# Forget sums by DMA, memory keys ahead of the conv mixer's projections, and sixteen more conv taps on TensorE, with a new order of the work behind them

## The reference

```python
log_f = jax.nn.log_sigmoid(fl.astype(jnp.float32) + b_forget.astype(jnp.float32))
cum = jnp.cumsum(log_f, axis=1).transpose(0, 2, 1)        # 8 heads x 512
...
    sb = (jnp.einsum('bhqd,bhkd->bhqk', sl(qb), kb).astype(jnp.float32) * scale
          + (c_q[..., None] - cum[:, :, None, :]))
    pb = jax.nn.softmax(jnp.where(causal, sb, -jnp.inf), axis=-1)
...
def pool_conv_mixer(h, w_in, pool_w, pool_scale, dw_w, dw_b, ln_g, ln_b, w_out):
    z = h @ w_in
    u, glu_a, glu_b = jnp.split(z, [POOL_W, POOL_W + CONV_W], axis=-1)
    pooled = jnp.stack([window_mean_minus_self(ug[:, :, i], w)
                        for i, w in enumerate(POOL_WINDOWS)], axis=2)
    ya = jnp.einsum("btgc,gcd->btgd", pooled, pool_w).reshape(b, t, POOL_W) * pool_scale
    gl = glu_a * jax.nn.sigmoid(glu_b)
    cv = causal_dwconv(gl, dw_w) + dw_b                   # 512 channels, 31 taps
    yb = jax.nn.silu(layernorm(cv, ln_g, ln_b))
    return jnp.concatenate([ya, yb], axis=-1) @ w_out
def memory_cross_attention(h, m, wq, wkv, wo):
    k, v = jnp.split(m @ wkv, 2, axis=-1)
...
```

## Time and profile before

| | us |
|---|---|
| median of 3 runs (lowest, highest) | 2516.14 (2513.30, 2516.99) |
| profiled execution | 2517.59 |
| its span | 2515.8 |
| PE busy in the span | 2422.4 (96%) |
| DVE, ACT, POOL busy | 1255.4, 962.2, 1002.8 |

### The profile page before, as it was taken

One profiled execution on the slowest core, in us unless ns is written; L12 is line 12 of the kernel. 1 busy time (PEld: TensorE's weight loads), 2 busy tenths in 40 slices (PEclk: granted clock), 3 DMA queues, 4 the chain that ended last, 5 costly groups with the idle time before them and its releaser, 6 DMA issues.

```text
span 2515.8 us, 30042 instructions
## 1 busy us (share of the span) xinstructions
PE 2422.4 (96%) x11158; PEld 1914.9 (76%) x11158; DVE 1255.4 (50%) x2109; ACT 962.2 (38%) x1439; POOL 1002.8 (40%) x744
## 2 busy tenths in 40 slices
PE   7999999999999999888999999999989999999998
PEld 6777667977888887756868888887556987888887
DVE  4453544324333336795347555556764324555555
ACT  4354334433322225523344222225766433322223
POOL 3323324242444453553515554454121142445443
PEclk9999999999999999998999999999999999999999
DMA  5222113431323222221312323222102331322331
GB/s 165 68 67 68 51 50 117 134 101 45 111 100 100 87 97 84 80 88 51 108 47 84 104 98 100 92 92 73 44 18 84 126 109 34 101 90 95 100 101 67
DMA packets 175563, 215.74 MB, mean 86 GB/s; under 512 B 6432, under 2 KB 157522, under 8 KB 175446
## 3 DMA queue, kind: packets, MB, share of 16 engines
q1 hardware_dynamic: 175446, 214.16, 26.2%
HBM read 212.04 MB, written 2.11 MB: 85 GB/s over the span
## 4 chain that ended last, share of the span: by engine, by line
PE 85%; DVE 9%; ACT 3%; issue 2%; POOL 1%; DMA 1%; DVEq 0%; SPq 0%; ACTq 0%
PE ps_l L771 74%; DVE arena L2327 3%; PE ps_l L984 3%; PE ps_l L1113 2%; PE ps_s L1040 2%; PE ps_l L893 2%; ACT w_hi L1306 1%; PE ps_s L1096 1%; POOL w_lo L622 1%; DVE arena L1852 1%; DVE a_lo L1858 1%; PE ps_s L999 1%; DVE x_T L2168 0%; DVE small L2546 0%; ACT arena L1333 0%
## 5 line engine op out<-in xcount | busy, mean ns | idle before, releaser
L622 POOL TENSOR_TENSOR w_lo<-w_raw,w_hi 128x512 fp32r<-128x512 f32 (+1 forms) x740 | 1002.6, 1387 | 1486.7 <-ACT w_hi L1306 1476.6
L771 PE MATMUL ps_l<-a_hi,w_hi 128*128 128x512 f32 x1936 | 768.3, 397 | 25.7 <-DVE b_lo L2186 16.0
L771 PE MATMUL ps_l<-a_lo,w_hi 128*128 128x512 f32 x1952 | 763.3, 392 | 0.0
L771 PE MATMUL ps_l<-a_hi,w_lo 128*128 128x512 f32 x1936 | 757.9, 391 | 0.0
L1306 ACT ACTIVATE w_hi<-w_raw 128x2048 fp32r<-128x2048 f32 x197 | 372.4, 1890 | 579.0 <-PE ps_l L771 560.3
L771 PEld LDWEIGHTS ps_l<-a_hi,w_hi 128*128 128x128 f32 x1936 | 366.1, 189 | 111.9 <-DVE b_lo L2186 16.7
L771 PEld LDWEIGHTS ps_l<-a_lo,w_hi 128*128 128x128 f32 x1952 | 369.6, 189 | 79.1 <-issue 2.9
L771 PEld LDWEIGHTS ps_l<-a_hi,w_lo 128*128 128x128 f32 x1936 | 365.5, 189 | 78.3
L771 PE MATMUL ps_l<-b_hi,w_hi 128*128 128x512 f32 (+1 forms) x908 | 337.1, 371 | 11.5 <-POOL w_lo L622 6.8
L771 PE MATMUL ps_l<-b_lo,w_hi 128*128 128x512 f32 (+1 forms) x908 | 334.8, 369 | 0.0
L771 PE MATMUL ps_l<-b_hi,w_lo 128*128 128x512 f32 (+1 forms) x908 | 334.8, 369 | 0.0
(11 more groups left out here) (272 smaller groups left out, 2629.3 us busy)
## 6 DMA issues: line engine op xcount, KB each, us to landing
w_raw<-in_ffn_w_up_dram SPq DMA_DIRECT2D x44, 1024.0 KB, 5.1
w_raw<-in_w_dram SPq DMA_DIRECT2D x32, 1024.0 KB, 5.2
w_raw<-in_ffn_w_down_dram SPq DMA_DIRECT2D x22, 1024.0 KB, 4.8
w_raw<-in_w_in_dram SPq DMA_DIRECT2D x20, 1024.0 KB, 5.4
w_raw<-in_xa_wkv_dram SPq DMA_DIRECT2D x16, 1024.0 KB, 5.6
w_raw<-in_w_kv_mem_dram SPq DMA_DIRECT2D x8, 1024.0 KB, 5.7
w_raw<-in_xa_wq_dram SPq DMA_DIRECT2D x8, 1024.0 KB, 5.0
w_raw<-in_xa_wo_dram SPq DMA_DIRECT2D x8, 1024.0 KB, 5.6
```

Of the source, the lines that this page charges most:

```text
L622: e.tensor_tensor(w_lo[:, b % 2, o], w_raw[:, b % 2, o], w_hi[:, b % 2, o].bitcast(F32), ALU.subtract).then_inc(w_lo_made[by], 1)
L771: ins = pe.matmul(o, *((v, w) if swap else (w, v)), start=first and n == 0, stop=last and n == 2)
```

## The change

1. **Forget sums.** The K matmuls and DVE's copies go. ACT writes `cum` to a DRAM buffer once, in its diff attention, and at each K event issues a DMA that reads one row of it back, broadcast to 128 partitions, into `nck`. DVE waits for it ahead of a head's first score.
2. **Memory keys.** `mem_rstd(1)` moves on ACT into the end of the MLP's loop; turns 0 and 1 of the memory stand ahead of the MLP's last projection, 2 and 3 behind it; three key blocks stand ahead of the sums and of glu, the fourth behind pool_u. ACT's and DVE's steps for them move with them (`last_z_and_keys`, `mem_keys` on DVE in two halves).
3. **Conv.** Of chunk 2, DVE does 15 taps and PE 16 (`conv2`), with the diagonals of `conv3` rewritten by ACT as they have been read. DVE adds the bank of conv2 to its own sum. DVE's taps fall from 93 to 77 and the counts at which it turns to other work are new.
4. **Order behind.** pc_out_a's second block stands between ln_mean and ln_var, and the four value blocks stand together behind ln_var. ACT and DVE follow.

The engines' rows, each in its program's order; the names are out<-in, and xN counts like rows.

ACT at the start of fox attention, before: the last high part of diff attention (L1466), then the exponentials of head 0 (L1499).

The diff, cut:

```diff
@@ -271,19 +270,23 @@
         for f in range(nf):
             if f + 1 < nf:
                 ups(f + 1)
+            elif name == "mlp":
+                L.add("memT1", "vv")
             put(down, 2, 1024, 256 * f, 0, "v" * 8)
         L.base[name + "_last"] = len(L.who) - 8
     mlp("mlp", FF1 // 256, [("w1", 0, "v")], "v", "w2")
     norm(3)
     norm(4, "v")
+    L.add("memT1+", "vv")
+    feat("xk1", "xa_wkv_2:0", "a", [0, 256, 512])
     feat("glu", "pc_w_in_2", "v", [512, 1024, 768, 1280])
-    L.add("memT1", "vvvv")
     feat("pool_u", "pc_w_in_2", "v", [0, 256])
-    keys(1, "xa_wkv_2:0")
+    feat("xk1+", "xa_wkv_2:0", "a", [768])
     L.add("pool_w", "vvvv")
     feat("pc_out_a", "pc_w_out_2", "v", [0, 512], nk=4, width=512)
     S.add("conv3", "v")
+    S.add("conv2", "v")
     S.add("ln_mean", "v")
     S.add("ln_var", "a")
     for j in range(4):
...
@@ -321,15 +324,17 @@
 TWO_PI = (6.28125, 2029 * 2.0 ** -20, 2 * np.pi - 6.28125 - 2029 * 2.0 ** -20)
 PI32 = 3.1415925
 PE_Q = 3
+SHARED_Q, SHARED_TAPS = 2, 15
 def tap_order():
...
@@ -1026,12 +1035,6 @@
                       turned=causal_turn(U["diff"], lambda h, i: s_diff(i, 0)), subln=diff_subln,
                       fills={"qk_b": feat_fill("qk_b", 8, 256, xa), "v_b": tok_fill("v_b")})
-            def fox_keys(g, h):
-                claim(pe, S, g)
-                pe.wait_ge(cum_ready, 2)
-                pe.matmul(bank(S, g)[:, :], ident[0:8, h:h + 1].to_broadcast([8, P]), cum, start=True, stop=True)\
-                    .then_inc(s_full, 1)
-
             def masked_score(g, i, pairs):
...
@@ -1149,6 +1152,9 @@
                     if f + 1 < nf:
                         ups(b, g)
                         down(f, b + n_up, g + 2 * n_up)
+                    elif name == "mlp":
+                        mem_turn(1, (0, 1))
+                        down(f, b, g + 2)
                     else:
                         down(f, b, g)
@@ -1159,16 +1165,20 @@
                 norm(3)
                 norm(4)
-            stage("glu", xa, ready=h_ready(4), behind={0: both_sums})
-            mem_turn(1)
+            mem_turn(1, (2, 3))
+            mem_keys(1)
+            both_sums()
+            stage("glu", xa, ready=h_ready(4))
             stage("pool_u", xa, nb=2)
-            mem_keys(1)
+            stage("xk1+", xm, nb=1, n=MEM)
             g = S.base["conv3"]
             claim(pe, S, g)
             pe.wait_ge(glu_r, 4)
             for j in range(CONV_K):
                 pe.wait_ge(diag_r, j + 1)
                 ins = pe.matmul(bank(S, g)[:, :], diag(j), gl[:, PE_Q, j:j + T], start=j == 0, stop=j == CONV_K - 1)
+                if j < CONV_K - 1:
+                    ins.then_inc(diag_read, 1)
             ins.then_inc(s_full, 1)
             g = L.base["pool_w"]
             pe.wait_ge(ld_pw, 16)
@@ -1177,23 +1187,30 @@
                 pe.wait_ge(pool_r, q + 1)
                 pe.matmul(bank(L, g + q)[:, :], pool_wt[:, q, :], window[q][:, 16:UW], start=True, stop=True)\
                     .then_inc(l_full, 1)
...
-            stage("pc_out_a", lambda k: xa(4 + k), nk=4, c=512, nb=2,
-                  ready=lambda k: wait_read(pe, L, L.base["pool_w"] + k))
+            g = S.base["conv2"]
+            claim(pe, S, g)
+            for j in range(SHARED_TAPS, CONV_K):
+                pe.wait_ge(diag_r, CONV_K + j - SHARED_TAPS + 1)
+                ins = pe.matmul(bank(S, g)[:, :], diag(j - SHARED_TAPS), gl[:, SHARED_Q, j:j + T],
+                                start=j == SHARED_TAPS, stop=j == CONV_K - 1)
+            ins.then_inc(s_full, 1)
+            b, g = plan.block_base["pc_out_a"], L.base["pc_out_a"]
+            feat(b, g, 4, 512, lambda k: xa(4 + k), lambda k: wait_read(pe, L, L.base["pool_w"] + k))
             g = S.base["ln_mean"]
             claim(pe, S, g)
             pe.wait_ge(tap, TAPS)
-            wait_read(pe, S, S.base["conv3"])
+            wait_read(pe, S, S.base["conv2"])
             for q in range(4):
                 ins = pe.matmul(bank(S, g)[:, :], ones[:, :], cvt[:, q, :], start=q == 0, stop=q == 3)
             ins.then_inc(s_full, 1)
-            mem_values(1, 0)
+            feat(b + 1, L.base["pc_out_a"] + 4, 4, 512, lambda k: xa(4 + k))
             g = S.base["ln_var"]
             claim(pe, S, g)
             for q in range(4):
                 pe.wait_ge(ln_sq, q + 1)
                 ins = pe.matmul(bank(S, g)[:, :], ones[:, :], ly[:, q, :], start=q == 0, stop=q == 3)
             ins.then_inc(s_full, 1)
-            for j in (1, 2, 3):
+            for j in range(4):
                 mem_values(1, j)
             stage("pc_out_b", xa, nk=4, c=512, nb=2, ready=lambda k: pe.wait_ge(yb_lo, k + 1))
             cross(1, 5)
...
@@ -1431,6 +1448,15 @@
                 act.activation(pt(h)[:, 0:i + 1, i * P:(i + 1) * P], tiles, ACT.Copy).then_inc(l_free["a"], 1)
+            def sums_row(h):
+
+                act.wait_ge(ld_sums, 16)
+                if h < 2:
+                    act.wait_ge(sub_n, 3 + h)
+                else:
+                    wait_read(act, S, plan.events["fox"][1]["S", h - 2, TT - 1])
+                act.dma_start(nck[:, h % 2, :], sums_d[h:h + 1, :].to_broadcast([P, T])).then_inc(ld_sums, 16)
...
@@ -1453,6 +1479,9 @@
                     copy_turned(g, h, i)
                 if kind == "O":
                     wait_group(act, L, g)
+                    if h == 0:
+                        act.wait_ge(cum_ready, 2)
+                        act.dma_start(sums_d, cum).then_inc(ld_sums, 16)
                     if h >= 2:
                         wait_group(act, S, at["M", h - 2, 0])
...
                     square(k, n, g)
-            def mlp(k_norm, after):
+            def last_z_and_keys():
+
+                g = L.base["mlp_last"]
+                mem_parts(1, range(4))
+                for n in range(KD - 1):
+                    z_hi(4, n, g)
+                hi(plan.block_base["xk1"] + 1)
+                mem_parts(1, range(4, KD))
+                z_hi(4, KD - 1, g)
+                for n in range(KD):
+                    square(3, n, g)
+                    square(4, n, g)
+                    if n in (1, 5):
+                        key_copies(1, n // 4)
+                key_copies(1, 2)
+
+            def mlp(k_norm):
                 b0, g0 = plan.block_base["mlp"], L.base["mlp"]
                 norm_rstd(k_norm)
                 u = UPB["mlp"]
...
+
+            def shared_diags():
+
+                for j in range(SHARED_TAPS, CONV_K):
+                    act.wait_ge(diag_read, j - SHARED_TAPS + 1)
+                    w = COL["conv_dw_w_2"] + 4 * j + SHARED_Q
+                    act.activation(diag(j - SHARED_TAPS), ident, ACT.Copy, scale=cols[:, w:w + 1]).then_inc(diag_r, 1)
             g, b = L.base["glu"], plan.block_base["glu"]
             for pair in (0, 1):
...
@@ -2334,19 +2396,18 @@
             glu_in(1, 1)
             taps(18)
             glu(1)
-            mem_keys(1)
             normed_x(range(4, KD))
             scaled(L.base["pool_u"], 2, lambda j: up_[:, j, 16:UW], r34)
+            taps(26)
+            scaled(L.base["pool_u"] + 2, 2, lambda j: up_[:, 2 + j, 16:UW], r34)
             taps(28)
-            scaled(L.base["pool_u"] + 2, 2, lambda j: up_[:, 2 + j, 16:UW], r34)
-            taps(40)
             wait_read(dve, L, L.base["pool_u"] + 3)
             for n, (dst, src) in enumerate(((pw_a, up_), (pw_b, pw_a[:, 1:4]), (pw_a[:, 2:4], pw_b[:, 1:3]),
...
@@ -2355,7 +2416,7 @@
             for q, w in enumerate(WINDOWS):
                 dve.scalar_tensor_tensor(out=window[q][:, 16:UW], in0=window[q][:, 16:UW], scalar=1.0 / w,
                                          in1=up_[:, q, 16:UW], op0=ALU.mult, op1=ALU.subtract).then_inc(pool_r, 1)
-            taps(76)
+            taps(60)
             for q in range(4):
                 g = L.base["pool_w"] + q
                 wait_group(dve, L, g)
...
                                          in1=A_hi[:, 4 + q, :].bitcast(F32), op0=ALU.mult, op1=ALU.subtract)\
                     .then_inc(l_free["v"], 1)
-            dve.wait_ge(x_normed, 8)
-            for n in range(KD):
-                taps(76 + 2 * (n + 1))
-                g = L.base["pc_out_a"] + n
-                wait_group(dve, L, g)
-                dve.tensor_tensor(x[:, n, :], bank(L, g)[:, :], x[:, n, :], ALU.add).then_inc(l_free["v"], 1)
             taps(TAPS)
             g = S.base["conv3"]
             wait_group(dve, S, g)
             dve.tensor_scalar(cvt[:, PE_Q, :], bank(S, g)[:, :], col("conv_dw_b_2", PE_Q), None, ALU.add)\
                 .then_inc(s_free["v"], 1)
+            g = S.base["conv2"]
+            wait_group(dve, S, g)
+            dve.wait_ge(tap, TAPS)
+            dve.tensor_tensor(cvt[:, SHARED_Q, :], cvt[:, SHARED_Q, :], bank(S, g)[:, :], ALU.add)\
+                .then_inc(s_free["v"], 1)
+
+            def pool_out(ns):
+                for n in ns:
```

(7 more changed lines are left out.)

130 lines of the change are left out of this document (71 added, 59 removed).

## The result

The changed kernel takes 2480.54 us (median of four runs, 2478.91 to 2481.74) where the kernel before takes 2515.32 beside it: 34.8 us less, a ratio of 0.986 with a 95% interval of 0.985 to 0.987. The prediction was 2484, with 2476 to 2497 as its range. The profiled execution took 2479.44 us, its span 2477.5, against 2517.59 and 2515.8.

What follows compares the result with a forecast made beforehand. PE's own queue bounds the fox stretch; the conv stretch is PE work plus waits, mostly on DVE's tap queue, and half clock. Fox -8.4 and conv -23.8 give -32.2 us: median 2516.14 to 2484, range 2476 to 2497.

Steps and rivals of the forecast that it cites:

- Fox sums: Fox attention: eight K events leave PE's full queue at 1.05 us each, 8.4 us gained.
- the cover: Fox attention: slack of 13.0 us before DVE reads head 1's row and 10.4 behind; PE waits from 23.4.
- The landing: Fox attention: time from issue until a broadcast row arrives, 2.9 or 5.2 us, with 5.2 taken as nearer.
- Head: Start of the conv stretch, keys ahead of sums: PE waits 1.7, 0.8 and 2.4 us; the 8.1 us keys' wait goes.
- one spell: Conv stretch: one spell of PE at half clock, 1.7 us (none to two: 0 to 3.4).
- Conv, PE: Conv stretch: sixteen taps move from DVE to PE at 0.86 us each, adding 13.7 us of PE work.
- Conv, DVE: Conv stretch: DVE's queue of 47.7 us plus 15.7 beside POOL; margins one to two before pool_w, 3 before ln_mean.
- Rival B: Conv stretch: DVE stays the bound, all 20 POOL pieces cost it 1.27 us; 2488 to 2496 us, chance 0.26.
- Behind: Behind the conv, pc_out_a to xv3: PE waits of 1.6, 0.4 and 0.8 us, where before had 2.1 and 0.8.
- Sum: Conv stretch: PE work 177.8 + 13.7, waits 7.7, spell 1.7, together 200.9 against 224.7 us; with fox -32.2.

Runs made afterwards that it cites:

- the kernel with the old order: Changed kernel with the whole old order behind the conv on PE, ACT and DVE; sums by DMA, keys at the head and conv2 stay: 2494.05 us.
- conv taps only: Kernel before with only the 16 taps of chunk 2 on PE behind pool_w, nothing else moved: 2510.20 us, ratio 0.9975.
- sums and keys: Kernel before with forget sums by DMA and keys at the head, all conv taps on DVE and old order behind: 2498.34 us, ratio 0.9932.
- both of the old order: Changed kernel with the old order behind the conv, put back on PE alone (2490.34 us) or on PE, ACT and DVE (2494.05 us).
- the kernel with late rows: Changed kernel with each head's row issued only directly ahead of that head's first exponential: 2479.38 us, ratio 0.9857.
- the kernel with 14 taps: Changed kernel with 17 taps of chunk 2 on DVE and 14 on PE, instead of 15 and 16: 2479.76 us, ratio 0.9855.

## Why the prediction was right

**Fox sums, -8.4.** The term is exact, the cover as read. The landing I had placed near 5.2 us was 3.0 to 3.4.

**Head.** I had waits of 1.7, 0.8 and 2.4 us; they are 1.5, 0.7 and 1.8, at the same three places and with the same releasers, and no spell of half clock follows. The sum had its one spell, 1.7 us, here behind the sums' wait, since I took POOL's 2.3 us as the shortest wait of before that a spell followed. That was misread: xv3's 7.52 us in the earlier trace rows follow a wait of 2.08, as the timeline of the kernel before has it:

```profile
1194.04 0.39 PE L771 MATMUL ps_l<-w_hi,b_hi 128*128 128x256 f32 x1 [2.08 <-POOL w_lo L622]
```

ACT's mem_rstd fits into its idle time: it ends at 946.1, with the next operand waited for behind it, and PE doesn't wait.

**Conv, PE.** conv2 took 13.9 us for 13.7 forecast, ln_mean and ln_var 3.60 each.

**Conv, DVE.** From the first gate product to the last window product I had 63.4 us, and it took 64.4 (1030.29 to 1094.75). I counted 15 or so POOL pieces beside it; all 20 were, at 0.8 us each on average, 17 in all. It left 0.6 us of margin ahead of pool_w instead of 1 to 2, and 2.9 instead of 3 ahead of ln_mean. The timeline of DVE in the changed kernel:

```profile
1072.74 6.78 DVE L2389 SCALAR_TENSOR_TENSOR arena<-arena,cols 128x512 f32<-128x512 f32 x4
...
1082.22 2.73 DVE L2389 SCALAR_TENSOR_TENSOR arena<-arena,cols 128x512 f32<-128x512 f32 x4
```

and of POOL:

```profile
1044.41 17.63 POOL L633 TENSOR_TENSOR w_lo<-w_raw,w_hi 128x512 fp32r<-128x512 f32 x8 [6.29 <-ACT w_hi L1323]
1065.20 15.44 POOL L633 TENSOR_TENSOR w_lo<-w_raw,w_hi 128x512 fp32r<-128x512 f32 x8 [3.16 <-ACT w_hi L1323]
```

The first piece of the 17.63 us, in a window of its own:

```profile
1044.41 6.43 POOL L633 TENSOR_TENSOR w_lo<-w_raw,w_hi 128x512 fp32r<-128x512 f32 x1 [6.29 <-ACT w_hi L1323]
```

Four taps take 6.78 us beside POOL and 2.73 without, and POOL's eight pieces 15.44 and 17.63 us where four alone take 5.03: each side is held up by the other. Beside taps the two go one for one, a tap and a piece in 1.70 us, so that a tap loses 1.0 us. Beside DVE's window addition of 3.43 us a piece takes 3.38. And the first piece of the 17.63 us takes 6.43, while DVE's queue beside it (taps and two gate products) goes on at 0.67 us an operation for 5.3 us and loses nothing there: so the average is 0.8 and not 1.0. The Trainium skill says on its page "SBUF — State Buffer", section "Who interferes with whom", that the shared ports are an exclusive lock, for a DVE operation with two SBUF inputs too. The trace agrees in kind and not in size: a piece alone (1.26) and a tap alone (0.67) one after the other would take 1.93 us, and the pair takes 1.70. Where the 0.2 us overlap no run here shows. Rival B, which made each piece cost DVE 1.27, didn't come.

**Behind.** Waits of 2.08, 0 and 0.78 against 1.6, 0.4, 0.8, and a spell of 1.2 us at xv2, where I had none (xv2 and xv3 take 13.26 us, xv0 and xv1 before them 12.07):

```profile
1154.93 0.38 PE L782 MATMUL ps_l<-w_hi,b_hi 128*128 128x256 f32 x1 [2.08 <-POOL w_lo L633]
```

So one spell was forecast and one came, at another place and behind another wait: that this term of the sum is nearly right is luck.

**Sum.** The stretch took 199.5 us for the 200.9 forecast; the waiting came out 0.8 smaller in all and the spell 0.5 shorter. By the start of pc_out_b the forecast of -32.2 stands against -33.4. The rest, 1.4 us of the measured 34.8 and 4.9 of the 38.3 between the two profiled spans, is the clock in latent attention, which no term held; the range had room for it. In the second traces of the two kernels it is 3.9.

**What the right number hid.** The sum costs the new order behind by its waits only and gives it no value of its own. The experiments show that it is the part on which most hangs: without the order 13.4 us are lost (11.7 without the spell at the sums), without conv2 9.4. Step by step the stretch's 25.2 us come, rounded, as 7.4 for the keys with the sums, 8.5 for the order and 9.4 for conv2. In another order of the steps the shares are others: conv2 brings 2.7 in the kernel before, 4.5 with the keys moved, and 9.4 with keys and order. DVE works in order, and each wait in its queue holds the taps behind it, as the kernel with the old order shows. My own expectations for the single edits missed four times (conv taps only, sums and keys, and both of the old order), while the sum for the whole came out; it was made on the whole new timeline and not part by part.

## What to carry to other kernels

When an engine that works strictly in order carries filler work (here the taps) between reads that wait for another engine, moving a stage on that other engine moves the waits, and the filler behind them stands still: put the filler ahead of the first read that can wait, and order both engines in one edit. Cost a change of several edits on one timeline of the changed program, stage by stage, and don't add up the worth of its parts. When a gain of 2 to 4 us doesn't show in the total, look for the same waits with and without half clock further down before giving it up.

## What the runs showed of the hardware

A single-input DVE operation is slowed by POOL too: eight scalings of 128 x 512 by a column take 9.24 us beside POOL's low parts in the changed kernel, where the same eight take 3.18 in the kernel before, with POOL idle, and a read of PSUM with one SBUF input isn't: two take 1.27 us beside POOL and 1.29 alone. The Trainium skill, on the page and in the section named above, lists tensor_scalar among the operations that can take the shared pair of ports in a two-port mode; the trace agrees.

The scalings in the kernel before:

```profile
994.21 3.18 DVE L2282 TENSOR_SCALAR x_T<-x_T,cols 128x512 f32<-128x512 f32 x8
```

in the changed kernel, with two reads of PSUM once POOL is idle:

```profile
994.99 9.24 DVE L2344 TENSOR_SCALAR x_T<-x_T,cols 128x512 f32<-128x512 f32 x8
...
1008.29 1.29 DVE L1951 TENSOR_TENSOR arena<-ps_l,arena 128x512 f32<-128x512 f32 x2
```

two such reads beside POOL:

```profile
1056.42 1.27 DVE L1951 TENSOR_TENSOR arena<-ps_l,arena 128x512 f32<-128x512 f32 x2
```

and POOL's pieces beside the scalings:

```profile
991.37 11.79 POOL L633 TENSOR_TENSOR w_lo<-w_raw,w_hi 128x512 fp32r<-128x512 f32 x8 [3.79 <-ACT w_hi L1323]
```

A row of 2 KB, read from DRAM and broadcast to 128 partitions, is usable 3.1 us after its issue on ACT's queue in the changed kernel, and 3.0 to 3.4 us after it in all eight heads of the kernel with late rows; its issue takes 0.33 to 0.36 us of the sequencer. And a wait of 2.1 to 2.2 us in the same place of the same code was followed by half clock in eight traces of fourteen and by none in six. A wait of 1.8 us was followed by none in both traces of the changed kernel, and by half clock in the kernel with 14 taps and in the one with the old order, whose code up to there is the changed kernel's.
